# Splitting all 34 mixing panels of each layer into high and low parts, where eight were multiplied whole

## What is computed

```python
z = h @ w_in[l]                                   # 1024 x 6400
q, k, v, u, gates = jnp.split(z, SPLITS, axis=-1)
q = apply_rope(q, cos, sin); k = apply_rope(k, cos, sin)
# three groups of four heads, dilated causal windows, merged by their softmax denominators
y_attn = o @ attn_wo[l]
a, g = jnp.split(u, 2); h = a * sigmoid(g)        # GLU
h = depthwise_conv(h, conv_w)  (31 taps) + conv_b
y_conv = silu(layer_norm(h)) @ conv_wo[l]
y = sigmoid(g_attn) * y_attn + sigmoid(g_conv) * y_conv
x = x + gate(1) * (y @ w_out[l])
```

## Time and profile before

| | |
|---|---|
| median of 3 runs | 1379.12 us (1378.84 to 1379.25) |
| the profiled execution: span from first to last instruction | 1379.0 us |
| TensorE matmul busy | 94% |
| TensorE weight load busy | 91% |
| DVE busy | 75% |
| ACT busy | 42% |

### The profile page before, as it was taken

The page is one execution under the profiler, slowest core; times in us unless marked ns, Lnnn a source line. Parts: engine busy times, 40 slices in busy tenths (PEclk is TensorE's granted clock), DMA queues, the critical chain, the costliest instruction groups (busy, mean ns, idle before and its releaser), DMA issues.

```text
span 1379.0 us, 24125 instructions
## 1 busy us (share of the span) xinstructions
PE 1297.4 (94%) x9992; PEld 1254.2 (91%) x9992; DVE 1035.6 (75%) x1220; ACT 573.8 (42%) x619; POOL 37.4 (3%) x50
## 2 busy tenths in 40 slices
PE   2699999899999899999989999989999989999997
PEld 1699999899888889999989999989988879899997
DVE  6998886798989766876577876678998976644444
ACT  2333334532335644443353333352323574533333
POOL 0010000000000010000000000000000000000000
PEclk8799999999999999999999999999999999999999
DMA  9989995335434366987827988623452525455550
GB/s 375 339 291 371 373 351 174 105 108 188 132 122 160 115 229 208 371 303 277 319 93 269 370 280 280 202 91 124 152 184 68 180 89 189 145 185 183 182 182 31
DMA packets 182600, 289.28 MB, mean 210 GB/s; under 512 B 4240, under 2 KB 163088, under 8 KB 176272
## 3 DMA queue, kind: packets, MB, share of 16 engines
q1 hardware_dynamic: 176784, 225.58, 48.9%
q0 software_dynamic: 5760, 62.92, 12.3%
HBM read 287.43 MB, written 1.05 MB: 209 GB/s over the span
## 4 chain that ended last, share of the span: by engine, by line
PE 78%; DVE 12%; ACT 4%; DMA 4%; issue 1%; SPq 0%; DVEq 0%; ACTq 0%
PE ps L386 23%; PE ps L387 23%; PE ps L388 23%; PE ps L422 5%; DVE work L1132 4%; DVE w_lo L938 3%; DMA raw<-in_w_in 2%; ACT w_hi L747 2%; PE ps L439 1%; DVE rstd L955 1%; DMA arena<-in_ada_w 1%; PE ps L450 1%; DVE arena L1277 1%; DMA raw<-in_ffn_wg 1%; PE ps L433 1%
## 5 line engine op out<-in xcount | busy, mean ns | idle before, releaser
L386 PE MATMUL ps<-hA_hi,w_hi 128*128 128x256 f32 x2016 | 581.5, 288 | 24.6 <-DVE hA_lo L974 20.4
L938 DVE TENSOR_TENSOR w_lo<-raw,w_hi 128x2048 fp32r<-128x2048 f32 x184 | 421.6, 2291 | 206.0 <-ACT w_hi L753 140.9
L387 PE MATMUL ps<-hA_lo,w_hi 128*128 128x256 f32 x2016 | 575.7, 286 | 0.0
L388 PE MATMUL ps<-hA_hi,w_lo 128*128 128x256 f32 x2016 | 575.6, 286 | 0.0
L386 PEld LDWEIGHTS ps<-hA_hi,w_hi 128*128 128x128 f32 x2016 | 392.4, 195 | 31.7 <-issue 29.4
L387 PEld LDWEIGHTS ps<-hA_lo,w_hi 128*128 128x128 f32 x2016 | 392.5, 195 | 0.2
L388 PEld LDWEIGHTS ps<-hA_hi,w_lo 128*128 128x128 f32 x2016 | 392.3, 195 | 0.0
L753 ACT CAST w_hi<-raw 128x2048 fp32r<-128x2048 f32 x108 | 206.4, 1911 | 245.6 <-PE ps L388 245.6
L1132 DVE SCALAR_TENSOR_TENSOR work<-conv_in,par,work 128x256 f32<-128x256 f32 x480 | 194.4, 480 | 0.0
L747 ACT CAST w_hi<-raw 128x2048 fp32r<-128x2048 f32 x76 | 144.4, 1904 | 112.8 <-PE ps L388 51.3
L386 PE MATMUL ps<-mid_hi,w_hi 128*128 128x256 f32 x672 | 187.2, 279 | 0.0
(11 more groups left out here) (102 smaller groups left out, 1108.0 us busy)
## 6 DMA issues: line engine op xcount, KB each, us to landing
arena<-in_ada_w POOLq DMA_DIRECT2D x40, 1536.0 KB, 6.7
raw<-in_w_in SPq DMA_DIRECT2D x50, 1024.0 KB, 5.6
raw<-in_ffn_wg SPq DMA_DIRECT2D x44, 1024.0 KB, 7.5
raw<-in_ffn_wu SPq DMA_DIRECT2D x44, 1024.0 KB, 6.0
raw<-in_ffn_wd SPq DMA_DIRECT2D x44, 1024.0 KB, 4.9
arena<-in_ada_w SPq DMA_DIRECT2D x12, 1024.0 KB, 10.3
raw<-in_conv_wo SPq DMA_DIRECT2D x8, 1024.0 KB, 6.7
raw<-in_w_out SPq DMA_DIRECT2D x8, 1024.0 KB, 5.0
```

The costliest lines, as they stand in the source:

```text
L386: nc.tensor.matmul(out_ap, stat[0], mov[0], start=start, stop=False, **kw)
L387: nc.tensor.matmul(out_ap, stat[0], mov[1], start=False, stop=False, **kw)
L388: return nc.tensor.matmul(out_ap, stat[1], mov[0], start=False, stop=stop, **kw)
L938: return nc.vector.tensor_tensor(dst, whole, hi_part.bitcast(F32), ALU.subtract)
```

## The change

The list of whole panels becomes empty, so that all 34 panels of a mixing sub-layer are split. Nothing else is edited.

```diff
-WHOLE = (4, 7, 10, 12, 15, 18, 20, 22)
+WHOLE = ()
```

## The result

| | median of 4 runs | lowest to highest |
|---|---|---|
| before | 1378.98 us | 1378.84 to 1379.25 |
| changed | 1392.63 us | 1392.22 to 1393.41 |

The ratio is 1.0101, with a 95% interval of 1.0088 to 1.0113: the change makes the kernel 13.65 us slower. Forecast were 1390 (+10.8), 1387 to 1392.5 about it, and a range of 1385.5 to 1396.5; the median lies in the range and 0.1 us above the inner band. The profiled execution of the changed kernel took 1392.22 us and has a span of 1390.5 us, 11.5 more than that of before.

What follows compares the result with a forecast made beforehand. TensorE was taken to set the pace with DVE close behind, both nearly full. Delays of 6.0 us in layer 0 and 4.8 in layer 1 added 10.8 to 1379.1, giving about 1390, range 1385.5 to 1396.5.

Steps and rivals of the forecast that it cites:

- What bounds: From panel 3's subtraction to the last mask, TensorE sets the pace, DVE close behind with about 15 us room a layer.
- What TensorE saves, 18.2 us: A split panel takes 1.14 us less than a whole one, 18.2 us for 16, counting only where TensorE arrives last.
- DVE's waits one by one: Layer 0: 17.6 us of new subtractions, 11.6 us recovered from waits and starts, so last mask 6.0 us later.
- Layer 1: Panel 3 to last mask grows from 159.7 us to 164.5, the same list length as layer 0: 4.8 us delay.
- Casts at nothing: ACT's eight added casts a layer cost nothing; its busy time in the stretch rises from 51.0 to some 69 us.
- Where TensorE rests: TensorE rests about 6 us at the third rotation and nearly 3 us before head 0's scores, which start at 377.9.
- Rival 1, the clock: TensorE's clock falls in the new rests, slowing head 0's scores and panel 17 by 1.7 to 2.5 us a layer; chance 0.2.
- The sum: Whole kernel: 6.0 us in layer 0 plus 4.8 in layer 1, 10.8 us added to 1379.1.
- rival 2: TensorE keeps setting the end, subtractions lie beside matmuls, and 18.2 us come off: 1360.9; chance 0.03.
- rival 3: DVE keeps its 6.8 us of waits among the heads, 6 us a layer more: 1402; chance 0.07.
- rival 4: DVE uses all its room, with panel 4's cast in time and no waits among heads: 1383 to 1386; chance 0.1.

## Why the prediction was right

- *What bounds.* Right: two engines nearly full, DVE with some 15 us of room a layer. Half the taps turn the change from 13.65 us slower to 16.8 us faster, which shows DVE's list as the cause.
- *What TensorE saves, 18.2 us.* Right for a panel: a split one between heads took 5.85 us to the transposes again (396.73 to 402.58). As a whole it was never had. With half the taps, where DVE leads least, 13.6 us show up to the column sums; that the medians lie 16.8 us apart is in part luck.
- *DVE's waits one by one.* The wait ahead of panel 4 was forecast at 2.4 us and measured 2.19 and, in layer 1, 2.39; the waits for later casts are gone in layer 0 and in layer 1; of the waits among the heads 0.66 us are left, where 0.8 was kept. The last mask came 5.6 us later in layer 0, where 6.0 was forecast, and the column sums began at 446.96, where 447.4 was.
- *Layer 1.* The list is 164.19 us long, where 164.5 was forecast. Its difference to before, 4.5 against 4.8 forecast, held in the profiled executions. But the forecast took the one profiled layer 1 of before for the rule, and in the pair with the zeros ahead of the sums the two layers cost the same, 5.6 and 5.7 us. So that the 4.8 came out is in part luck.
- *Casts at nothing.* No wait for a cast is left past panel 4, with ACT at 66.7 us of 164.2 (forecast some 69 busy). The run with ACT's and DVE's part only cannot part the two engines, so "nothing" rests on the waits alone.
- *Where TensorE rests.* The scores of head 0 started at 377.63 (forecast 377.9). The split of the rests was wrong: 4.08 us ahead of the third rotation instead of about 6, and nearly none ahead of the scores instead of 3 (in layer 1 4.12 and 1.18). It had no wait of TensorE for a subtraction, and there are 2.5 us of these. The clock had fallen already at the second rotation, behind rests of 0.94 and 1.02 us, so panel 15 began slow, and so did panel 16. The path didn't move, since all of this lies in the wait for DVE: DVE's last rope step begins at 376.75 us in layer 0 and the scores 0.88 us behind it, in layer 1 0.74 us behind it.
- *Rival 1, the clock.* Its mechanism is real, and its place was wrong. The reason given against it, that the second rest is shorter than one of 3.23 us that once passed without a fall, didn't hold: the clock fell behind rests of 0.94 and 1.02 us. Around the rotations it costs nothing that these runs can tell (1392.17 with all rests filled), though it cost some 4 us in all where it was pushed to panel 17. Ahead of the layer norm's sums of layer 0, which the prediction held to be as before, it cost 1.4 us.
- *The remainder.* The sum was 10.8 and the runs grew by 13.65. The span grew by 11.5 us: 5.6 and 4.5 from DVE's list and 1.4 from the clock at those sums, a term that the sum didn't hold. In every kernel profiled here whose time is known the time was 1.65 to 1.79 us over the span. If that held for the profiled execution of before too, it was at 1380.7, some 1.7 us over its median, and that would account for most of the 2.1 us between. Its own time isn't known, so this is argued and not shown. The prediction put the span of before, 1379.0, equal to the median of its runs and took the 0.1 us between them for agreement.
- *Rivals 2 to 4.* That the work lies beside matmuls (rival 2) came true only with half the taps. Of DVE's waits neither more (rival 3) nor none (rival 4) were kept.

## What to carry to other kernels

When a change moves work from the busiest engine to the second, don't compare busy shares; go through the second engine's waits in the stage, in order, ask of each whether its cause goes away, and subtract only those. Work that saves 1.1 us on the one and costs 2.2 us on the other is a gain only where the other waits, so it can pay at one panel and cost at the next: the list of six whole panels was 6 us faster than that of eight and 20 us faster than the empty one. And a rest that is harmless on the path can still lower TensorE's clock for what follows it, so look at what runs behind each new rest.

## What the runs showed that was not expected

- The clock fell behind short rests. In the changed kernel TensorE rested 1.76 us ahead of 330.98 us and 0.94 and 1.02 us at the second rotation, some 20 us later; behind these the first matmuls of panel 15 followed each other after 0.21 us, until 357.0 us. In the kernel before, rests of 0.41 and 1.02 us at the third rotation lowered nothing: panel 16 took its 0.12 us a matmul behind them.
- Filling some rests made the kernel no faster and rather slower (1396.56 against 1392.63 us): the lower clock then came at work on the path, and with that rest filled too the loss was gone (1392.17).
- 13 matmuls of zeros in a rest of 3.2 us made the layer norm's sums take 3.69 us in the two layers where they took 3.69 to 6.63 otherwise, and took 2.4 us off the median of the kernel before in its group.
